# Rotary halves swapped by small transfers instead of a product with a rotation matrix

## The reference

```
def partial_rotary(x, positions):
    half = ROPE_DIM // 2                      # 16
    ang = positions[..., None] * inv_freq
    xr = x[..., :ROPE_DIM]
    x1, x2 = xr[..., :half], xr[..., half:]
    rot = concatenate([x1 * cos - x2 * sin, x2 * cos + x1 * sin])
    return concatenate([rot, x[..., ROPE_DIM:]])

z = rmsnorm(h, g_mix) @ w_in
q, k, v, u, gates = split(z)
q = partial_rotary(q, positions); k = partial_rotary(k, positions)
```

## Time and profile before

| | before |
|---|---|
| median of the runs | 1506.48 us |
| span of the profiled execution | 1505.74 us |
| TensorE matmul busy | 1428.6 us (95%), 10534 instructions |
| VectorE busy | 952.1 us (63%), 1132 instructions |
| ScalarE busy | 612.7 us (41%), 729 instructions |
| GpSimd busy | 392.8 us (26%), 302 instructions |
| rotation products (L2271) | 24 records, 92.4 to 202.4 us |

### The profile page before, as it was taken

The page is one execution under the profiler, slowest core; times in us unless marked ns, Lnnn a source line. Parts: engine busy times, 40 slices in busy tenths (PEclk is TensorE's granted clock), DMA queues, the critical chain, the costliest instruction groups (busy, mean ns, idle before and its releaser), DMA issues.

```text
span 1505.7 us, 24502 instructions
## 1 busy us (share of the span) xinstructions
PE 1428.6 (95%) x10534; PEld 1239.9 (82%) x10534; DVE 952.1 (63%) x1132; ACT 612.7 (41%) x729; POOL 392.8 (26%) x302
## 2 busy tenths in 40 slices
PE   5899999979999999998899999999999998899999
PEld 5888899979999996763577888888886965899999
DVE  6888765566768666858738777255415578586333
ACT  5623445343344364533623322322223447433433
POOL 4975703000004400000002343442320010034553
PEclk9999999999999999999999999999999999999999
DMA  7542334556676565853536654344333400465552
GB/s 249 170 141 85 113 111 139 186 181 203 217 237 224 172 220 180 234 176 85 175 102 210 193 179 156 126 145 149 121 102 113 168 29 2 140 224 171 193 170 82
DMA packets 156084, 236.15 MB, mean 157 GB/s; under 512 B 6577, under 2 KB 126417, under 8 KB 155857
## 3 DMA queue, kind: packets, MB, share of 16 engines
q1 hardware_dynamic: 152336, 230.78, 46.5%
q10 hardware_dynamic: 3648, 3.92, 1.1%
HBM read 227.55 MB, written 1.05 MB: 152 GB/s over the span
## 4 chain that ended last, share of the span: by engine, by line
PE 82%; DVE 8%; POOL 5%; ACT 3%; issue 2%; DMA 1%; DVEq 0%; SPq 0%; ACTq 0%; POOLq 0%
PE bank L2119 24%; PE bank L2120 23%; PE bank L2121 23%; PE bank L2429 2%; DVE wlo L1163 1%; PE bank L2183 1%; POOL X L1973 1%; PE bank L2597 1%; PE bank L2586 1%; PE bank L617 1%; PE bank L2262 1%; DVE stat L1858 1%; PE bank L2308 1%; DMA A<-in_w_mod 1%; PE bank L2271 1%
## 5 line engine op out<-in xcount | busy, mean ns | idle before, releaser
L2119 PE MATMUL bank<-ahi,whi 128*128 128x256 f32 (+1 forms) x2480 | 792.4, 320 | 23.7 <-DVE alo L1630 4.9
L2120 PE MATMUL bank<-alo,whi 128*128 128x256 f32 (+1 forms) x2480 | 782.5, 316 | 0.0
L2121 PE MATMUL bank<-ahi,wlo 128*128 128x256 f32 (+1 forms) x2480 | 782.1, 315 | 0.0
L1163 DVE TENSOR_TENSOR wlo<-raw,whi 128x2048 fp32r<-128x2048 f32 x160 | 367.5, 2297 | 357.2 <-ACT whi L689 356.8
L689 ACT ACTIVATE whi<-raw 128x2048 fp32r<-128x2048 f32 x160 | 306.3, 1914 | 658.6 <-PE bank L2121 658.5
L2119 PEld LDWEIGHTS bank<-ahi,whi 128*128 128x128 f32 x2480 | 476.4, 192 | 71.4 <-issue 26.6
L2121 PEld LDWEIGHTS bank<-ahi,wlo 128*128 128x128 f32 x2480 | 476.6, 192 | 28.7
L2120 PEld LDWEIGHTS bank<-alo,whi 128*128 128x128 f32 x2480 | 476.8, 192 | 26.9 <-issue 0.2
L2086 POOL TENSOR_TENSOR A<-A 128x512 f32 (+1 forms) x48 | 106.8, 2238 | 480.0 <-ACT A L1029 480.0
L2068 POOL TENSOR_TENSOR alo<-A,ahi 128x512 fp32r<-128x512 f32 (+1 forms) x43 | 126.5, 2945 | 354.3 <-ACT ahi L895 354.3
L1524 DVE SCALAR_TENSOR_TENSOR A<-modraw,scc,A 128x1024 f32<-128x1024 f32 x70 | 121.3, 1772 | 0.6
(11 more groups left out here) (306 smaller groups left out, 1219.6 us busy)
## 6 DMA issues: line engine op xcount, KB each, us to landing
raw<-in_w_ff SPq DMA_DIRECT2D x64, 1024.0 KB, 5.2
modraw<-in_w_mod SPq DMA_DIRECT2D x72, 512.0 KB, 4.6
raw<-in_w_in SPq DMA_DIRECT2D x28, 1024.0 KB, 5.1
A<-in_w_mod SPq DMA_DIRECT2D x24, 512.0 KB, 5.3
raw<-in_pw SPq DMA_DIRECT2D x12, 1024.0 KB, 6.6
raw<-in_w_ffn_gate SPq DMA_DIRECT2D x11, 1024.0 KB, 5.3
raw<-in_w_ffn_up SPq DMA_DIRECT2D x11, 1024.0 KB, 5.4
raw<-in_w_ffn_down SPq DMA_DIRECT2D x11, 1024.0 KB, 5.1
```

The source lines that it names most:

```text
L1163: dve.tensor_tensor(wlo[:, k % 2, :], raw[:, (k + 2) % 4, :], whi[:, k % 2, :].bitcast(F32), ALU.subtract).then_inc(wlo_ready, 1)
L2119: pe.matmul(out_, w_hi, a_hi, start=start, stop=False, **kw)
L2120: pe.matmul(out_, w_hi, a_lo, start=False, stop=False, **kw)
L2121: return pe.matmul(out_, w_lo, a_hi, start=False, stop=stop, **kw)
```

## The change

The rotation product is taken out of TensorE's program, with its semaphore `rot_done`. Instead SyncE issues, behind load(l) for l = 14 to 25, two transfers for the pair n = l - 14: partitions 16 to 31 of the pair go to partitions 0 to 15 of a small buffer, and 0 to 15 to 16 to 31. Each moves 16 partitions x 512 f32. They wait until the pair's block has been copied out and, from the third pair on, until `rotate(n-2)` has used the buffer. There are two buffers, the second in `rstd`. VectorE's `rotate` waits for both transfers, multiplies the swapped halves by the sine table in place, and goes on as before. The sign of the first half moves into the sine table: its Sin takes a scale of -1 or 1 by partition from a new constant. Three semaphores that nothing waited for go away too, and `turn_probs(1)` no longer waits for the rotations.

```diff
+        rotb = [t.rearrange("p (a t) -> p a t", a=2) for t in (msk[0:32, 1152:1664], rstd[0:32, 0:512])]
+        def rotary_part(n):
+            t, m = (q_s if n < 6 else k_s), n % 6
+            return t[0:32, 2 * m:2 * m + 2, :]
...
+                        if Q0 <= l - 6 < GATE0:
+                            n = l - 6 - Q0
+                            sync.wait_ge(evac["in"], Q0 + n + 1)
+                            if n >= 2:
+                                sync.wait_ge(roped, n - 1)
+                            for a in range(2):
+                                sync.dma_start(rotb[n % 2][16 * a:16 * a + 16],
+                                               rotary_part(n)[16 - 16 * a:32 - 16 * a]).then_inc(rot_landed[n % 2], 16)
...
-                act.activation(rope[0:32, 1, :], posw[:, 1, :], ACT.Sin).then_inc(sin_out, 1)
+                act.activation(rope[0:32, 1, :], posw[:, 1, :], ACT.Sin, scale=C["rotsign"][0:32, :]).then_inc(sin_out, 1)
...
-                dve.wait_ge(rot_done, n + 1)
-                dve.tensor_tensor(rotb, pb[3][0:32, :].rearrange("p (a t) -> p a t", a=2), sbb, ALU.mult)
+                dve.wait_ge(rot_landed[n % 2], 32 * (n // 2 + 1))
+                dve.tensor_tensor(swapped, swapped, sbb, ALU.mult)
                 link(dve.tensor_tensor(part, part, cb, ALU.mult))
-                dve.tensor_tensor(part, part, rotb, ALU.add).then_inc(roped, 1)
+                dve.tensor_tensor(part, part, swapped, ALU.add).then_inc(roped, 1)
...
-            def rotation(n):
-                t, m = (q_s if n < 6 else k_s), n % 6
-                pe.wait_ge(evac["in"], Q0 + n + 1)
-                if n >= 1:
-                    pe.wait_ge(roped, n)
-                pe.matmul(pb[3][0:32, :], C["rotg"][0:32, 0:32], t[0:32, 2 * m:2 * m + 2, :],
-                          start=True, stop=True).then_inc(rot_done, 1)
...
-                if n == 1:
-                    pe.wait_ge(roped, 12)
...
-                if Q0 <= l - 1 < GATE0:
-                    rotation(l - 1 - Q0)
```

More of the change, by code:

```diff
@@ L101 @@
 MOD_COLLECT = [0, 1, 6, 7, 8, 9, 11]
-CONSTS = [("ident", 128), ("ones", 128), ("halves", 128), ("rotg", 128), ("invf", 1),
+CONSTS = [("ident", 128), ("ones", 128), ("halves", 128), ("rotg", 128), ("invf", 1), ("rotsign", 1),
           ("gmix", 8), ("gffn", 8), ("gfinal", 8), ("convb", 8), ("lng", 8), ("lnb", 8), ("g1", 16), ("g2", 16),
@@ L172, in program @@
         p1, p2 = msk[:, 0:512], msk[:, 512:1024]
-        rotb = msk[0:32, 1152:1664].rearrange("p (a t) -> p a t", a=2)
+        rotb = [t.rearrange("p (a t) -> p a t", a=2) for t in (msk[0:32, 1152:1664], rstd[0:32, 0:512])]
+        def rotary_part(n):
+            t, m = (q_s if n < 6 else k_s), n % 6
+            return t[0:32, 2 * m:2 * m + 2, :]
         powers = msk[:, 1664:1920].rearrange("p (n s j) -> p n s j", n=8, s=2)
@@ L269, in program @@
         scc_ready = sem("scc_ready")
-        silu_ready = sem("silu_ready")
         sin_in = sem("sin_in")
         sin_out = sem("sin_out")
-        rtab_ready = sem("rtab_ready")
         tab_ready = sem("tab_ready")
@@ L293, in program @@
         ylo_ready = sem("ylo_ready")
-        rot_done = sem("rot_done")
+        rot_landed = [sem(f"rot_landed{n}") for n in range(2)]
         roped = sem("roped")
@@ L314, in program @@
         hlo_ready = sem("hidden_lo_ready")
-        x_ready = sem("x_ready")
         phi_ready = sem("p_hi_ready")
@@ L1252, in _ @@
             dve.wait_ge(scc_ready, 1)
-            dve.tensor_tensor(scc[:, 0:16], scc[:, 0:16], C["cc"], ALU.mult).then_inc(silu_ready, 1)
+            dve.tensor_tensor(scc[:, 0:16], scc[:, 0:16], C["cc"], ALU.mult)
             dve.wait_ge(pos_landed, 16)
@@ L1357, in rotate @@
             def rotate(n):
-                t = q_s if n < 6 else k_s
-                m = n % 6
-                part = t[0:32, 2 * m:2 * m + 2, :]
+                part, swapped = rotary_part(n), rotb[n % 2]
                 cb = rope[0:32, 0, :].unsqueeze(1).broadcast_to([32, 2, T1])
@@ L2679, in constants @@
             masks.append(np.where(ok, 0.0, NSCORE).astype(f))
-    return dict(ident=np.eye(P, dtype=f), ones=np.ones((P, P), f), halves=halves, rotg=rot, invf=invf), \
+    sign = np.ones((P, 1), f)
+    sign[:16] = -1
+    return dict(ident=np.eye(P, dtype=f), ones=np.ones((P, P), f), halves=halves, rotg=rot, invf=invf, rotsign=sign), \
         gtab, np.concatenate(masks, axis=1)
```

## The result

The changed kernel takes 1520.49 us (median of four runs, 1518.21 to 1525.80) beside 1506.63 us for the kernel before on the same chips. The ratio is 1.0087, with a 95% interval of 1.0066 to 1.0107: slower by 13 us, 10 to 16. I had forecast 1513.5 us, 7 us slower, and a range up to 1519. The direction and the ring hold; the size came out at twice what I forecast.

A forecast was written before the change was run, and what follows sets the result against it. VectorE and TensorE lead by turns to 144 us, then TensorE to 209. Span 1505.74 + 6.4 (block 21 late) + 0.7 (clock) = 1512.8, with 0.74 to the median 1513.5 us; range 1504 to 1519.

The forecast's parts named there:

- the ring: In the rotations: W, load issued, swaps issued, swaps landed, rotate(n), next W; one turn takes 10.1 us.
- W: W(k) is the time at which the low part of weight block k, VectorE's work, is ready.
- L: Time from W to both swaps landed: 5.5 us (2.9 to 6.9), as a load and small transfer at 589 us.
- W(15) 0.5 us late: Start of the rotations: W(13) 0.5 us late, then long SSM work hides the transfer, W(15) at 146.5.
- the turns: Four uncovered turns of the ring, n = 5 to 8, after W(15): 10.1 us each, W(19) at 186.9.
- 21.4 us from W(19) to W(21), covered: SSM and attention work covers the transfer or nearly so: 21.4 us as before, W(21) at 208.3, 9.0 us later.
- The path behind it: From W(21) to block 21 on TensorE: 7.3 us, so block 21 starts at 215.6, 6.4 us late.
- The waits: TensorE waits for VectorE at ssm_turn(3) and scores(1); VectorE waits 3 to 5 us at n = 0, 5 to 8.
- The clock: TensorE's granted clock may fall to 1.2 GHz after waits; only the last counts: 0 to 3.4 us, taken as 0.7.
- 9.3 us saved on TensorE: From 143.93 us on, eight products of 0.97 us and a 1.5 us wait removed, but swallowed by waits.
- Rival (a): Faster: the swap overtakes the load, L = 2.9, a turn is 7.5 us, 1502.1 us; chance 0.14.
- Rival (c): Slower still: swaps pay a full transfer behind the load, L = 6.9, 5.6 us more, 1519 us; chance 0.10.

The follow-up runs named there:

- experiments 1 and 7: Changed kernel with swaps issued just ahead of the load: 1505.29 us; changed kernel with each load cut in two, swaps between the halves: 1511.33 us.
- Experiment 5: Against the changed kernel, only pairs 0 to 4 swapped by transfers behind the load, the rest by the product on TensorE: 1512.23 us.
- Experiment 11: Changed kernel with idle products filling TensorE's waits (2, 7 and 4 at three places): 1523.44 us.
- experiment 12: Kernel of experiment 2, with GpSimd leaving out the last two of four state-power steps of the fourth group: 1500.68 us.
- experiment 2: Changed kernel with early swaps: issued ahead of the load and its wait, once the pair's block is copied out: 1504.06 us.
- Experiment 10: Against the kernel of experiment 2, pairs 0 to 4 by the product on TensorE, only pairs 5 to 11 by early swaps: 1504.79 us.
- experiment 6: Against the changed kernel, pairs 0 to 4 by the product on TensorE, only pairs 5 to 11 by transfers behind the load: 1520.23 us.
- experiment 9: Kernel of experiment 2 plus idle products in TensorE's waits, four ahead of ssm_y(0) and three ahead of ssm_turn(2): 1503.03 us.

## Why the prediction was wrong in size

**The ring.** Right, and shown: SyncE's load follows W within 0.03 us, the swaps follow the load, VectorE waits for them, and the next load waits for VectorE. Putting the swaps one place ahead removes it.

**L.** I took 5.5 us from the pair at 589 us. The pairs with no cover waited 5.60 (n = 5) and 5.68 (n = 8); for n = 6 and 7 the start lay 6.18 and 5.83 after W. The rule of the Trainium skill that I weighed ("DMA: Bandwidth & Descriptors", "Queues, rings and completion order": on each DMA engine descriptors are consumed in ring order) fits with experiments 1 and 7, where the wait fell to 2.55 us with nothing ahead of the swaps and to 4.16 with half a load. The worst pair fits too: at 102.75 us the load took 6.6 us to land instead of 5.1, its swaps 5.3 instead of 4.7, and `rotate(1)` started 7.05 us after W:

```profile
raw<-in_w_in SPq DMA_DIRECT2D x1, 1024.0 KB, 6.6
rstd<-A SPq DMA_DIRECT2D x2, 32.0 KB, 5.3
```

**The first step that failed: "W(15) 0.5 us late".** It was 2.7 late (148.68 against 145.99). I let three turns of 10.1 us stand for the start, and even their sum was misread: 91.99 + 3 x 10.1 = 122.3 is what my own middle values give, 1.3 us late, not the slow case (three turns with `rotate` at 2.70 give 123.4), and I took 0.5. The first turn took 10.7 and the second 12.0 (W(11) at 102.72, W(12) at 112.42 + 2.27 = 114.69): `rotate` took 2.9 and 2.7 us where I allowed 2.0 to 2.35, and with the slow load L was 7.05 instead of 5.5. W(13) was so 3.6 us late (122.34 + 2.27 = 124.61 against 120.97); up to W(15) 0.9 of it was made good. Experiment 5 prices this start at 5 us, and it brought TensorE's 8.5 us ahead of ssm_turn(2).

**The second: the turns.** From W(15) to W(19) it took 41.8 us (190.43 - 148.68) where I had 40.4, a third of a microsecond a turn. That is L: 5.61, 6.18, 5.83 and 5.68 us from W to the start of `rotate`, 1.3 us more than four times 5.5.

**The third: "21.4 us from W(19) to W(21), covered".** It took 22.8 (213.21 - 190.43): the attention step ahead of `rotate(10)` did not cover L, 1.75 us of idle time in the row at 209.02 where `rotate(10)` had waited 0.56 for its product before, and `rotate(9)` took 3.0 us instead of 2.3, with the other work half a microsecond shorter.

W(21) was so 13.9 us late instead of 9.0. The path behind it was right: 7.5 us to block 21 (220.70 - 213.21), 7.3 forecast. All of it falls under one fault: I took each term near its middle or its best row, and in a ring every excess adds up, because no slack is left between the turns. With L at its bound of 6.0 and `rotate` at 2.70 throughout, the sum would have reached past 1519. What was wrong is thus the size of terms, not the ring itself.

**The waits.** ssm_turn(3) and scores(1) waited as forecast (4.59 and 2.09 us). ssm_turn(2) I had not named, and it was the longest. n = 3 and 4 had no wait, right; n = 0 and 5 to 8 had theirs (2.44 us for n = 6 and up to 5.68 for n = 8, where I had said 3 to 5), and n = 1, 2, 10 and 11 too, which I had not listed.

**The clock.** It fell as I thought it might. In the wait ahead of ssm_turn(2) TensorE worked 0.75 of 7 us, and the next 4 us had its 1.2 GHz level:

```profile
133.00:140.00 7.00, 0.75 (x4) 0.78 (x5) 6.86 (x14) 0.23 (x1) 0.03 (x1) 0.60 0.08 18
140.00:144.00 4.00, 4.00 (x21) 4.00 (x20) 3.83 (x11) 1.09 (x2) 2.52 (x4) 0.50 0.74 251
```

It was absorbed ahead of block 21, as forecast: VectorE was waited for again behind it, at 171.10 and at 194.68. Experiment 11, which kept it up in part, won nothing. Only the last dip reached the path: weigh(0) took 1.16 us to block 21's first matmul (220.70 - 219.54) where it had taken 0.66, and block 21 began at the low level.

**"9.3 us saved on TensorE".** This fell as well, though the forecast did not rest on it. First, it was miscounted: the row at 143.93 us is the product n = 5, so seven products lie from there on, not eight, and the sum is 7 x 0.97 + 1.5 = 8.3 us. Second, free of the ring, they are worth 4 us; block 21 came 5.0 us early. Another 1.8 us stay with GpSimd (experiment 12), 1.0 of them as the wait ahead of weigh(0). The last 1.5 us lie in the rows of ssm_turn(2) and block 14: without the product ahead of them TensorE waits longer for VectorE, and then works at a lower clock: 9.4 us instead of 6.8 in experiment 2. With less work on GpSimd, too, block 15 started only 0.5 us early (148.82) of the 2.5 that were freed ahead of it. Experiment 10, which keeps the products there, has this loss no more and meets GpSimd's so much sooner. No run takes away both.

**Rival (a)** had 1502.1 us for L = 2.9; with 2.55 it came to 1505.3. Its ring was right, W(19) at 176.69 where it had 176.1; then W(20) came only at 190.45, 13.8 us later instead of 11.6, since the first maximum waited 0.87 us for GpSimd, and the scan ahead of it and `rotate(9)` took 0.7 us longer each. The break-even that I put at L = 3.9 us lies near 3.2: by the ratios the kernel gains 2 us at 2.55 and loses 3 at 4.16. **Rival (c)**, 1519 us, was nearest in time, but not by its mechanism: L was not 6.9, save in the one pair with the slow load.

**What stays open:** why the load at 102.75 us was slow; and what is left of TensorE's 8.3 us when neither GpSimd nor the lower clock of block 14 takes its part.

The kernel with early swaps beats both: 1504.06 us, 0.27% faster than before (0.12 to 0.42), and 17 us faster than the change as made, by moving eight lines up.

## What to carry to other kernels

A small transfer that somebody waits for must not stand behind a bulk load in the same queue: here its latency was that of the load, and one place in the order of issue was worth 15 us. Before adding such a wait, write down what triggers the transfer; if that is the work which the waiter does next but one, there is a ring, and its length is to be held against the time of a block, at its worst rows. Before a wait is taken out because it held nothing, as turn_probs(1)'s did in the kernel before, or left in for the same reason, ask what it would hold once its releaser comes late: in experiment 6 it was 2.7 us. And an engine's busy share of 99% does not say that every microsecond taken from it arrives: of 8.3 us 4 to 5 did, and GpSimd's wait grew with every gain ahead of it.

## What the runs showed of the hardware

Two transfers of 32 KB between SBUF regions, with nothing ahead of them in the queue, let VectorE go on 2.55 us after their trigger, issue of both included. GpSimd's small operations (128 x 256, 0.61 us) took up to 3.26 us when VectorE's 128 x 2048 subtraction ran at the same time (lengths on GpSimd are rough), in the kernel before (at 143.21 us) as in the changed one:

```profile
177.78 3.26 POOL L2028 TENSOR_TENSOR modrow<-A,sp 128x256 f32<-128x256 f32 x1
```

It stands beside the low part at 178.29 us; the next of its kind, at 182.63, took 0.61. After a wait of TensorE of 3.9 to 4.0 us the granted clock was 0.50, its 1.2 GHz level, from 136 to 139 us, with three idle products ahead of the wait (experiment 9) as without (experiment 2): ssm_turn(2) and block 14 behind it took 9.4 to 9.5 us instead of 6.8. Seven idle products in all brought the mean of the stretch from 0.84 to 0.93, and no time that can be told from none.
